# Masks moved from TensorE into VectorE's row minimum, and the order of waits, weight slots and stages changed, in a three-block transformer kernel

## The reference

```python
# forgetting attention: 16 heads of 64, blocks of 128 queries
s = q @ k.T * scale + c[q] - c[k];  p = softmax(where(key <= query, s, -inf));  o = p @ v
# third block, one input product split in 11 parts
I[t, s] = sum_h w[t, h] * relu(q_idx[t, h] . k_idx[s]) * scale         # index scores, 8 heads
sel     = top_k(where(s < chunk_limit(t), I, -1e30), 128)
o_a     = softmax(q_a . k_a over the selected keys) @ v_a               # 8 heads of 64, after norm and rope
q_b     = rope(norm(norm(c_q) @ w_uq));  k_b, v_b from norm(c_kv) @ w_ukv and a rope key
o_b     = softmax(where(s < chunk_limit(t), q_b . k_b, -1e30)) @ v_b    # 8 heads
h       = h + concat(o_a * silu(g_a), o_b * silu(g_b)) @ w_out
```

## Time and profile before

| what | us |
|---|---|
| median of 3 runs (1829.71 to 1834.44) | 1830.02 |
| profiled execution | 1825.58 |
| its span | 1823.8 |
| PE busy | 1760.4 |
| ACT, DVE, POOL busy | 661.3, 627.6, 680.8 |
| last product ends | 1819.5 |

### The profile page before, as it was taken

One profiled execution on the slowest core, in us unless ns is written; L12 is line 12 of the kernel. 1 busy time (PEld: TensorE's weight loads), 2 busy tenths in 40 slices (PEclk: granted clock), 3 DMA queues, 4 the chain that ended last, 5 costly groups with the idle time before them and its releaser, 6 DMA issues.

```text
span 1823.8 us, 24023 instructions
## 1 busy us (share of the span) xinstructions
PE 1760.4 (97%) x9646; PEld 1486.3 (81%) x9646; DVE 627.6 (34%) x1080; ACT 661.3 (36%) x996; POOL 680.8 (37%) x522
## 2 busy tenths in 40 slices
PE   5999999899999999999999999999999899999999
PEld 5777889688888888888899888888888787888777
DVE  2449425240100011542356320100013538993341
ACT  3643624242222223523334332222223445435540
POOL 2524333244444455442400254444553434352002
PEclk9999999999999999999999999999999999999999
DMA  4212111222222223221300122223222222121001
GB/s 184 70 47 82 59 70 45 106 70 98 101 100 103 92 94 107 87 106 71 116 1 1 47 93 92 102 105 119 92 92 93 93 93 93 69 93 47 1 1 46
DMA packets 23203, 145.08 MB, mean 80 GB/s; under 512 B 3504, under 2 KB 4144, under 8 KB 7120
## 3 DMA queue, kind: packets, MB, share of 16 engines
q1 hardware_dynamic: 23120, 143.90, 22.2%
HBM read 141.72 MB, written 2.10 MB: 79 GB/s over the span
## 4 chain that ended last, share of the span: by engine, by line
issue 39%; PE 31%; POOL 23%; DVE 4%; ACT 2%; DMA 1%; POOLq 0%; SPq 0%; ACTq 0%; DVEq 0%
POOL wlo L2509 23%; PE PS L460 3%; PE PS L462 3%; PE PS L461 3%; PE PS L1603 2%; PE PS L936 1%; PE PS L549 1%; PE PS L550 1%; PE PS L551 1%; PE PS L1576 1%; DVE cva L576 1%; PE PS L328 1%; PE PS L331 1%; PE PS L323 1%; PE PS L1592 1%
## 5 line engine op out<-in xcount | busy, mean ns | idle before, releaser
L2509 POOL TENSOR_TENSOR wlo<-wraw,whi 128x512 fp32r<-128x512 f32 (+2 forms) x500 | 662.5, 1357 | 1089.6 <-ACT whi L134 1089.6
L134 ACT ACTIVATE whi<-wraw 128x2048 fp32r<-128x2048 f32 (+2 forms) x125 | 235.3, 1882 | 238.2 <-PE PS L331 192.9
L427 PE MATMUL PS<-hT_hi,whi 128*128 128x512 f32 x704 | 274.0, 389 | 0.0
L428 PE MATMUL PS<-hT_lo,whi 128*128 128x512 f32 x704 | 273.9, 389 | 0.0
L429 PE MATMUL PS<-hT_hi,wlo 128*128 128x512 f32 x704 | 273.9, 389 | 0.0
L1514 DVE TENSOR_TENSOR act_sb<-sil,PS 128x512 f32 x44 | 30.3, 688 | 428.6 <-ACT sil L1490 428.6
L1490 ACT ACTIVATE sil<-PS 128x512 f32<-128x512 f32 x44 | 26.3, 598 | 355.3 <-PE PS L429 335.4
L427 PEld LDWEIGHTS PS<-hT_hi,whi 128*128 128x128 f32 x704 | 132.2, 188 | 27.5
L428 PEld LDWEIGHTS PS<-hT_lo,whi 128*128 128x128 f32 x704 | 132.2, 188 | 27.4
L429 PEld LDWEIGHTS PS<-hT_hi,wlo 128*128 128x128 f32 x704 | 132.1, 188 | 27.1
L460 PE MATMUL PS<-whi,hT_hi 128*128 128x512 f32 (+2 forms) x320 | 124.4, 389 | 6.1 <-POOL wlo L2509 4.6
(11 more groups left out here) (373 smaller groups left out, 3135.0 us busy)
## 6 DMA issues: line engine op xcount, KB each, us to landing
wraw<-wpack SPq DMA_DIRECT2D x125, 1024.0 KB, 4.9
gain<-gains SPq DMA_DIRECT2D x10, 512.0 KB, 6.1
x_sb<-x SPq DMA_DIRECT2D x8, 512.0 KB, 7.5
out<-x_sb SPq DMA_DIRECT2D x4, 512.0 KB, 2.6
csb<-consts SPq DMA_DIRECT2D x1, 768.0 KB, 6.7
vh<-vecs SPq DMA_DIRECT2D x1, 96.0 KB, 6.4
small<-vecs SPq DMA_DIRECT2D x1, 80.0 KB, 11.8
small<-vecs SPq DMA_DIRECT2D x5, 0.5 KB, 5.4
```

The lines of the kernel that those rows point to most:

```text
L134: act.activation(whi[q % 2][:, w], wraw[q % 2][:, w], ACT.Copy).then_inc(w_hi, 1)
L427: nc.tensor.matmul(o, whi[q][w], hT_hi[:, k, :], start=(k == 0), stop=False)
L428: nc.tensor.matmul(o, whi[q][w], hT_lo[:, k, :], start=False, stop=False)
L2509: p.tensor_tensor(wlo[q][:, a:b], wraw[q][:, a:b], whi[q][:, a:b].bitcast(F32), ALU.subtract).then_inc(w_lo, 1)
```

## The change

- Start: the constants are loaded in two parts (identity early, the rest behind x), x tile 1 ahead of the gain; ACT's root table is loaded by a dummy root; ACT turns tile 0 and tile 1 one behind the other; DVE goes in pairs; the first head uses the order of the later ones.
- GDN: `act_blocks(0)` later, `dve_values(8)` earlier, `dve_gated(3)` and `act_root(3)` ahead of the turned tile 2, slot 0 of the output product finished before slot 1, slots 2 and 3 by pieces.
- Attention: no mask product; DVE's row reduction is replaced by one instruction that computes mask - scores in place and its row minimum; the exponential has scale -1. In FOX the wait for the last heads stands behind the first turn and the fourth scores. FOX and MLA get mask rows in SBUF.
- Third block: new order of parts (qa before ckv, ka before ukv, index scores behind qa's tiles), slot order of cq, turns moved, 16 of 48 top-k rounds inside MLA (steps 8 to 23), three turns straight behind the attention, the last tile written in two halves. On DVE the sums for qb stand ahead of the index scores, qb is finished before the key latent, ka before kb.

The diff, condensed: statements of several lines and loops are drawn together.

```diff
 def act_first(self):
+    nc.scalar.activation(warm[:, 4:5], epsb[:, :], ACT.Sqrt)
     for t in range(TT):
         self.act_sq(t); self.act_rt(t)
-        if t:
-            if t <= 2: act_split(t - 1)
-            self.T.act_tile(t - 1)
-    self.T.act_tile(TT - 1)
+        if t == 1: act_split(0); self.T.act_tile(0); self.T.act_tile(1)
+        if t == 2: act_split(1)
+    self.T.act_tile(2); self.T.act_tile(3)
...
 load_x(0)
+s.dma_start(csb[:, 0:P], consts[:, 0:P])
+load_x(1)
 gain_load(0, None)
-s.dma_start(csb[:, :], consts)
-load_x(1)
 s.dma_start(wraw[0][:, :], wpack[4]); s.dma_start(wraw[1][:, :], wpack[5])
 load_x(2); load_x(3)
+s.dma_start(csb[:, P:NCONST], consts[:, P:NCONST])
...
 act_silu(6)
-act_blocks(0)
 act_tap(8)
 act_silu(7)
 (second half of act_decay)
 act_tap(10)
+act_blocks(0)
 act_silu(9)
...
 gout_slot(1, [0])
 gout_slot(0, [1])
-gout_slot(1, [1])
 gw(t, "o", 3, 1)
 GT.pe_tile(2)
+gout_slot(1, [1])
+GT.pe_tile(3)
 gout_slot(0, [2])
+gout_slot(0, [3])
 gout_slot(1, [2])
-GT.pe_tile(3)
-gout_slot(0, [3])
 gout_slot(1, [3])
...
 def pe_scores(self, u):
-    t.matmul(PS[:, b, 0:d], q, self.k(h, 0, i), start=True, stop=True)
-    t.matmul(PS[:, b, d:n], q, self.k(h, i, i + 1), start=True, stop=False)
-    t.matmul(PS[:, b, d:n], ident, m, start=False, stop=True)
+    t.matmul(PS[:, b, 0:(i + 1) * P], q, self.k(h, 0, i + 1), start=True, stop=True)
 def dve_max(self, u):
-    v.tensor_reduce(nm, PS[scores], AX_X, ALU.max, negate=True)
+    s = PS[scores]
+    v.tensor_tensor_reduce(out=s, in0=s, in1=self.mask(i), scale=-1.0, scalar=-MAX_NEG,
+                           op0=ALU.add, op1=ALU.min, accum_out=nm)
 def pe_attend(attentions, begun=0, before_turn=None):
     for n in range(len(w) + 3):
         if begun <= n < len(w): scores of unit n
+        if n == 3 and before_turn: before_turn()
         if 2 <= n < len(w) + 2: turn of unit n - 2
...
-DENSE = ["cq", "qi", "uq0", "uq1", "ckv", "qa", "ukv0", "ukv1", "ka", "va", "ga", "gb"]
+DENSE = ["cq", "qi", "uq0", "uq1", "qa", "ckv", "ka", "ukv0", "ukv1", "va", "ga", "gb"]
 def pe_second():
-    cq units (slot, tile): (0,0) (1,0) (0,1) T2 T3 (1,1) (0,2) (1,2) (0,3) (1,3)
+    cq units (slot, tile): (0,0) (0,1) (1,0) T2 T3 (1,1) (0,2) (0,3) (1,2) (1,3)
-    dense("ckv", index scores behind each tile)
-    dense("qa", {(0, 2): turns("Tckv")})
-    dense("ukv0"); dense("ukv1")
-    dense("ka", {(0, 1): turns("Tqb0"), (0, 3): turns("Tqb1")})
-    dense("va", {(0, 1): turns("Tqa"), (0, 3): turns("Tkb0"), (1, 1): turns("Tkb1")})
-    dense("ga", {(0, 3): turns("Tka")})
+    dense("qa", index scores behind each tile)
+    dense("ckv")
+    dense("ka", {(0, 2): turns("Tckv"), (1, 0): turns("Tqb0"), (1, 2): turns("Tqb1")})
+    dense("ukv0"); dense("ukv1")
+    dense("va", {(0, 1): turns("Tqa"), (0, 3): turns("Tka"), (1, 1): turns("Tkb0"), (1, 3): turns("Tkb1")})
+    dense("ga")
-    T2.pe(); pe_rows(OUT, "out2", T2)
+    T2.pe_tile(0..2); slot(0, [0]); T2.pe_tile(3); slot(0, [1, 2, 3]); ...; slot(3, [3], halves)
 def dve_second():
-    top(3 * ROUNDS - 17)
-    dve_attend([MLA, SPA])
+    top(2 * ROUNDS - 3)
+    dve_attend([MLA, SPA], lambda n: top(1) if 8 <= n < 8 + ROUNDS else None)
```

More of the change, by code:

```diff
@@ L209, in dve, with pe_first, pe_head @@
             def dve(self):
[L210 to L216, removed]
-                t, T = nc.tensor, self.T
[L220 to L239, removed]
+                for t in range(0, TT, 2):
+                    self.dve_xn(t)
+                    self.dve_xn(t + 1)
+                    self.T.dve(t)
+                    self.T.dve(t + 1)
+            def pe_first(self, n):
+                t, T = nc.tensor, self.T
+                T.pe_tile(0)
+                T.pe_tile(1)
+                self.pe_head(n, "row")
+            def pe_head(self, n, row=None):
+                t, T = nc.tensor, self.T
+                T.tile_done(t, 1)
+                feat_tile(n, 0, piece=True)
+                feat_tile(n + 1, 0, halves=(0,), piece=True)
+                T.pe_tile(2)
+                T.pe_tile(3)
+                feat_tile(n + 1, 0, halves=(1,))
+                T.tile_done(t, 3)
+                for m in range(2):
+                    feat_tile(n + m, 2, row)
         class Turn:
@@ L310, in mix_ready, with pe_slot @@
                     eng.wait_ge(w_used, self.b + self.ns)
-            def pe_slot(self, n, first, final, lhi, llo, ready=None, tiles=range(TT), piece=False):
+            def pe_slot(self, n, first, final, lhi, llo, ready=None, tiles=range(TT), piece=False, halves=False):
                 q = n % 2
+                if halves:
+                    self.pe_halves(n, lhi, llo, tiles[0])
+                    return
                 for t in tiles:
@@ L1978, in act_lat_squares @@
             evac_done(a, name, pair)
+            if name == "ckv":
+                a.wait_ge(sem("sums"), 2)
+                a.wait_ge(sem("root"), 2)
             for t in (2 * pair, 2 * pair + 1):
@@ L2321, in pe_second, with pe_out, ready, slot @@
             pe_attend([MLA, SPA], 3)
-            T2.pe()
-            pe_rows(OUT, "out2", T2)
+            pe_out()
+        def pe_out():
+            t = nc.tensor
+            def ready(tt):
+                T2.tile_done(t, min(tt + 1, 3) if tt else 0)
+            def slot(m, tiles, halves=False):
+                n = BASE["out2"] + m
+                if m < 3 or tiles[0]:
+                    low_ready(t, n)
+                OUT.pe_slot(n, m == 0, m == 3, lambda kk, tt: hT_hi[:, 2 * m + kk, tt * P:(tt + 1) * P],
+                            lambda kk, tt: hT_lo[:, 2 * m + kk, tt * P:(tt + 1) * P], ready if m == 0 else None, tiles,
+                            m == 3 and tiles[0] == 0, halves)
+            for tt in range(3):
+                T2.pe_tile(tt)
+            slot(0, [0])
+            T2.pe_tile(3)
+            slot(0, [1, 2, 3])
+            slot(1, range(TT))
+            for m, tt in ((2, 0), (2, 1), (3, 0), (3, 1), (2, 2), (3, 2), (2, 3)):
+                slot(m, [tt])
+            slot(3, [3], True)
         def act_second():
```

248 lines of the change are left out of this document (146 added, 102 removed).

## The result

The changed kernel takes 1811.6 us (median of four, 1809.2 to 1815.5) against 1829.9 beside it: ratio 0.9897, 95% interval 0.987 to 0.9923. That is 18 us faster, where 52 were forecast; the time lies outside the range. The profiled execution took 1809.2 us, its span is 1807.4.

The account below looks back on a forecast made before the run. PE's queue was taken as the bound (busy 97% of the span). Terms summed to 57.7 us, 52.2 after a clock discount of 5.5: from 1830.0 to 1778 us, 8-in-10 range 1764 to 1797.

Parts of the forecast that it names:

- the term of the masks for MLA and SPA: Attention stages MLA and SPA: taking mask products off PE, less the cost of top-k rounds in MLA, gains 4.3 us.
- Rival (b): Attention tails: with PE less loaded, units of i = 0 and 1 in MLA and SPA run at 1.2 GHz: 1794; 12%.
- my two signs of being wrong: DVE found without idle time in FOX, or PE waiting over 5 us in all at the turns of ka and kb.
- New DVE instruction: Attention masks on DVE: costs 0.15 us more than the plain reduction, 0.75 to 0.85 us for 512 columns.
- FOX: FOX attention: removing mask products gains 11.3 us; 2.2 us per unit at i = 3, 0.73 at i = 0.
- GDN output: GDN output product: three PE waits and a slow stretch go, taken as 10.5 us, bounds 6 and 10.7.
- tail: Kernel end: no wait for the last gated tile 2.9, halved last sum and store 0.8; 3.7 us in the sum.
- Start: Kernel start: first weight product 5.9 us earlier, plus a wait and a slow stretch gone; 9.2 us, bounds 5 and 10.5.
- Third block: Third block: waits for cq, at qi and L1938 with slow stretches go, less 1.5 for a slip; net 9.8 us.
- clock discount of 5.5: Whole kernel: 11 us of slow stretches assumed gone counted only half, since the clock also fell without long waits.
- The mask edit's worth at full clock: FOX, MLA and SPA: all mask terms 15.6 us after charging the top-k rounds 2.5; bounds 0 and 25.
- the rounds inside MLA: MLA: 16 top-k rounds on DVE cost 8 x 0.25 us at i = 2 and 0.5 at i = 1.

Follow-up runs that it names:

- 4: Changed kernel with all masks back on PE as identity products and plain maximum on DVE, in FOX, MLA and SPA: 1790.6 us, ratio 0.9802.
- 6: Changed kernel with the masks of MLA alone back on PE; FOX and SPA keep them on DVE: 1775.5 us, ratio 0.9699.
- 7: Changed kernel with the masks of MLA and SPA back on PE; only FOX has them on DVE: 1776.1 us, ratio 0.9707.
- run 8: Changed kernel plus unused PE products ahead of the wait for probabilities, in MLA's i = 2 to 0 and SPA's i = 1 and 0: 1770.5 us, ratio 0.9679.
- 11: Kernel before with the mask edit alone plus the idle products of run 8 in MLA and SPA: 1805.8 us, ratio 0.9883.
- 12: Changed kernel with the idle products of run 8 and the 16 top-k rounds in steps 3 to 18 instead of 8 to 23: 1768.0 us, ratio 0.9672.
- 14: Changed kernel with idle products of 512 columns only in MLA's i = 1 and 0, top-k rounds in steps 3 to 18: 1769.6 us, ratio 0.9681.
- run 5: Kernel before with only the mask edit (masks from PE into DVE's minimum in FOX, MLA, SPA): 1848.3, 1849.0, 1928.3 and 1928.6 us.
- control 13: Kernel before, masks on PE, with the idle products of run 8 added: 1831.6 us, ratio 1.0014.
- run 1: Changed kernel plus one unused product of the old mask product's shape in each SPA unit of i = 3 to 1: 1820.2 us.
- run 2: Changed kernel plus one burst of 16 unused 128x512 products ahead of the scores of SPA's first unit: 1777.5 us, ratio 0.971.
- run 3: Changed kernel with all 48 top-k rounds ahead of MLA, none inside it: 1815.7 us.
- run 9: Kernel of run 8 plus one pause: DVE copies a mask row eight times ahead of the minimum of SPA's third unit: 1814.0 us.
- run 10: Kernel of run 8 plus the same eight-copy DVE pause, ahead of the minimum of FOX's seventh unit: 1840.1 us.

## Why the prediction was wrong

**The step that failed** is the term of the masks for MLA and SPA, +4.3 us in the sum. It took the mask products out at their price at full clock, put the clock in both stages at 1.00, and left it there without a term. The ground was "at 1695 to 1704 the clock is 1.00 with waits inside", but that row was read with the mask products in, and the change takes them out. In its place the runs show a fall of the clock that begins in MLA and lasts through SPA, 105.7 us at 0.50: the two stages cost 37.3 us (5.6 + 31.7 in the ledger) where 4.3 were to be won. That the missing mask products bring it is shown by putting them back (runs 4, 6 and 7), by putting idle products in their place (8, 11, 12 and 14), by the mask edit alone (5), and by the control 13. With the clock held, run 8 takes 1770.5, and 1830.0 less the whole sum of 57.7 is 1772.3.

Rival (b), at 12%, had named the mechanism: "If the units of i = 0 and 1 in MLA and SPA run at 1.2 GHz, 32 units lose about 0.5 us each: 1794 too". Place, length and weight were not right. I treated the fall as local, like the stretches of 3.4 and 6.8 us of the earlier trace rows. Here it began in MLA's last units and struck SPA's i = 3 and 2, which I had as full of work, for 24 us (31.5 + 29.8 - 19.2 - 17.8), and i = 1 and 0 for 10. It fell in MLA in every traced run that had there neither mask products nor a substitute (after, 1, 2, 3, 5); where they or a substitute were there it fell in MLA once, for 3.4 us (6).

The mask product's 0.22 us per unit were counted as pure cost. In MLA they cost some 3 us in all (i = 3 to 0: 20.1, 16.6, 13.4 and 10.4 us in run 7, 18.8, 15.6, 13.1 and 9.7 in run 8) and kept the clock for the next stage. And of my two signs of being wrong neither showed (DVE is busy for 12.1 of 19.3 us in FOX's i = 3, PE waits 1.8 us at kb's turn): no sign watched the clock in MLA and SPA, where (b) needed one.

**Right, by size.** New DVE instruction: 0.15 us more, as taken. FOX: i = 3 at 2.19 us per unit (2.2 forecast), i = 0 at 0.76 (0.73), the stage 12.9 us shorter in run 5 from its first exponential to its last (108.2 and 95.3; 11.3 forecast). GDN output 11.2 (10.5), tail 3.2 (3.7): the wait for the last gated tile is gone and the last sum is half,

```profile
1804.30 0.69 DVE L2517 TENSOR_TENSOR x_sb<-x_sb,PS 128x512 f32<-128x512 f32 x1 [0.67 <-PE PS L351]
```

**Right by cancelling.** Start: the first product came at 17.06, not at 15.3. Tile 1's squares began at 7.87, not 6.2, and the gain behind two tiles of x now held up DVE's first scaling:

```profile
7.87 1.06 ACT L159 ACTIVATE junk<-x_sb 128x1024 f32<-128x1024 f32 x1 [1.67 <-DMA x_sb<-x]
...
9.73 1.28 DVE L193 SCALAR_TENSOR_TENSOR xn<-x_sb,small,gain 128x1024 f32<-128x1024 f32 x1 [3.34 <-DMA gain<-gains]
```

I had not charged the move of the gain load. So the first product came 4.2 us sooner (forecast 5.9), and from there to GDN another 4.6 us were won (forecast 3.6, by the earlier trace rows and the wait of 1.9): 8.8 for 9.2. Third block: cq and qi gave 8.0 (6.8 forecast), and what ukv gave (4.5) went again, 1.8 of it at kb's turn: sum 8.0 for 9.8. So that 50.5 met 49.7 so closely is in part luck. The clock discount of 5.5 was not needed outside attention: the five stretches counted went, three came there (17.6, 178.0 and 188.3, together 13.6 us), and three more of before went too (194.1, 235.0 and 999.6, 3.4 us each).

**Too small.** The mask edit's worth at full clock: 22.8 us in run 11, where the forecast's terms without the rounds are 18.1 (15.6 + 2.5). And the rounds inside MLA: against run 5, i = 2 and i = 1 are 1.3 and 2.9 us longer, but the second holds the 3.4 us at half clock. In run 8, at full clock, i = 1 is 1.8 us longer than in run 5, so the rounds took about 3.1 where I had 2.5. I had counted the round but not that once in eight units it meets the group's output and gate product, the queue of 2.3 us shown above.

**The rule on the accumulator** (the Trainium skill, page "VectorE: DVE Perf Modes", section "Two Vector instructions with no wait between them") holds here: two records, 141 ns for the second, less than ACT's 190. It is the 0.15 taken, and nothing came on top of it.

## What to carry to other kernels

When an edit takes work off PE in a stage that PE doesn't bound, price the clock of all that follows in stages of the same kind, not only the units that you changed: one pause with a wait of 2.1 us in SPA cost 43 us here, one with 1.7 us in FOX 70. Read the granted clock beside every busy share, because a PE at 1.2 GHz looks fully busy. If the stage must be thin, put idle products where PE waits anyway, ahead of the fall; the same products behind it did not raise the clock. And where the forecast leans on a row of the clock, ask whether that row was taken with the work in it that the change removes.

## What the hardware showed that was not expected

- In these attention stages the granted clock is a state with memory. SPA ran at 1.00 (burst, 54.5 us) or at 0.50 (105.7 us) with the same instructions; what came before decided. At 0.50 it stayed although PE was busy for 92.2 of 92.2 us (run 9). In SPA and FOX it never came back within the stage. What ended it was, in run 2, the 16 products of 128x512, and in all other runs the unbroken row of turns behind the stage (24 in the third block, 32 behind FOX), ahead of the first weight product: at 1758.4 in the changed kernel, whose turns run from 1755.7 to 1759.5, at 1759.2 in run 9, at 1034.3 in run 10. These turns have the shape of those inside the stage (128x128); what a row of them has that the stage lacks, no run separates.
- The Trainium skill, page "TensorE: Matmul & The Clock Gate", section "A second HAM failure mode: psum-queue depth-cycling", tells of short idle times between groups of products that make the clock swing between its two levels. A swing is seen here at MLA's end (1642.3 down, 1645.7 up, 1652.7 down); in SPA and FOX it did not swing but stayed down, for 92 to 150 us.
- Not settled is why MLA, without mask products, sometimes came back by itself (after 3.4 us in the changed kernel, 10.2 in run 3) and sometimes not (from 1632.1 in run 2, from 1641.9 in run 1), while SPA and FOX never did. Their score products use 96 rows of PE in MLA, 64 in SPA and 66 in FOX; no run varied that, nor which kinds of product hold the clock: both substitutes tried, mask products and idle ones, are plain products beside the turns and values.
- Single executions differ by where the fall in MLA comes: first at 1632.1 (run 2), 1641.9 (run 1) and 1642.3 (the changed kernel, which fell again at 1652.7), in kernels that are alike up to there. The later the fall, the less is lost before the burst of run 2, which would explain its spread (1772.4 to 1788.2); that is argued, since its other three executions have no trace.
